# Attention with shared keys: the last key tile's exponentials enter the summing product directly

## The reference, cut to what matters

```
def blocked_attention(q, k, v, scale):
    ...
        s = jnp.einsum('bqhgd,bkhd->bhgqk', qblk, k, preferred_element_type=jnp.float32) * scale
        p = jax.nn.softmax(s, axis=-1)
        return jnp.einsum('bhgqk,bkhd->bqhgd', p.astype(v.dtype), v)
...
        o = jnp.concatenate([
            blocked_attention(qm, ..., MLA_SCALE),
            blocked_attention(qg, ..., GQA_SCALE)], axis=-1)
```

## Time and profile before

| | |
|---|---|
| median of 3 runs | 3780.42 us (3778.26 to 3781.32) |
| the profiled execution, by the same clock as the runs | 3788.75 us |
| its span, first to last instruction | 3787.0 us |
| PE busy | 3304.8 us (87%) |
| DVE busy | 2715.6 us (72%) |
| ACT busy | 1853.9 us (49%) |
| mean granted TensorE clock | 0.936 |

### The profile page before, as it was taken

The page is one execution under the profiler, slowest core; times in us unless marked ns, Lnnn a source line. Parts: engine busy times, 40 slices in busy tenths (PEclk is TensorE's granted clock), DMA queues, the critical chain, the costliest instruction groups (busy, mean ns, idle before and its releaser), DMA issues. The chain is left out here.

```text
span 3787.0 us, 44337 instructions
## 1 busy us (share of the span) xinstructions
PE 3304.8 (87%) x14416; PEld 2224.1 (59%) x14416; DVE 2715.6 (72%) x2841; ACT 1853.9 (49%) x2125; POOL 1456.2 (38%) x1091
## 2 busy tenths in 40 slices
PE   6999699999695999999959996999978599999990
PEld 2555355544384788888824443555437488887870
DVE  1444466677586899989856654777767698988997
ACT  0222233344310888888823332333331188888881
POOL 2111011121111877777721110111121287777771
PEclk9999799999896999999979997999999699999995
DMA  8465532211441998798754336221115278997974
GB/s 339 157 233 186 157 94 67 58 48 37 143 150 71 404 365 309 275 350 321 298 210 135 124 102 181 73 64 43 40 39 196 98 292 336 349 363 284 353 276 195
DMA packets 258758, 739.56 MB, mean 195 GB/s; under 512 B 55456, under 2 KB 149440, under 8 KB 205272
## 3 DMA queue, kind: packets, MB, share of 16 engines
q0 software_dynamic: 114288, 528.57, 36.4%
q1 hardware_dynamic: 129816, 157.73, 13.7%
q10 hardware_dynamic: 14544, 51.92, 3.8%
HBM read 723.62 MB, written 129.61 MB: 225 GB/s over the span
## 5 line engine op out<-in xcount | busy, mean ns | idle before, releaser
L2033 DVE TENSOR_TENSOR ex_wl<-ex_wr,ex_wh 128x2048 fp32r<-128x2048 f32 x440 | 988.0, 2285 | 63.9 <-ACT ex_wh L1978 63.8
L1978 ACT ACTIVATE ex_wh<-ex_wr 128x2048 fp32r<-128x2048 f32 x440 | 843.1, 1916 | 77.4 <-PE ex_yp L1941 55.1
L1185 ACT ACTIVATE at_pt<-at_st 128x1024 f32<-128x1024 f32 (+1 forms) x336 | 336.5, 1003 | 552.7 <-PE at_st L1120 550.0
L1231 DVE TENSOR_REDUCE at_nm<-at_sc 128x1 f32<-128x1280 f32 (+1 forms) x276 | 378.3, 1371 | 216.1 <-PE at_sc L1085 213.6
L764 PE MATMUL zp<-w_in,hT 128*128 128x480 f32 x960 | 428.8, 580 | 31.5 <-DVE hT L539 21.6
L1245 DVE TENSOR_TENSOR at_acc<-at_acc,at_pt 128x1024 f32<-128x1024 f32 x256 | 318.2, 1243 | 94.6 <-ACT at_pt L1185 92.4
L1859 POOL DMA_INDIRECT ex_wr<-in_w_down,piece_of x152 | 315.6, 2077 | 46.3 <-issue 46.0
L1134 PE MATMUL at_op<-at_pt,at_va 128*64 128x512 f32 (+1 forms) x1344 | 318.6, 603 | 0.2
L1120 PE MATMUL at_st<-at_q,at_km 96*128 96x512 f32 (+3 forms) x1008 | 266.2, 404 | 16.6 <-DMA at_q<-at_nmT 14.6
L764 PEld LDWEIGHTS zp<-w_in,hT 128*128 128x128 f32 x960 | 173.5, 195 | 180.2 <-issue 168.5
L1120 PEld LDWEIGHTS at_st<-at_q,at_km 96*128 96x128 f32 (+1 forms) x1008 | 180.6, 193 | 104.0 <-issue 42.6
(11 more groups left out here) (281 smaller groups left out, 5941.2 us busy)
## 6 DMA issues: line engine op xcount, KB each, us to landing
ad_w<-in_w_ada POOLq DMA_DIRECT2D x48, 1024.0 KB, 10.4
q_mla<-qT SPq DMA_DIRECT2D x40, 384.0 KB, 3.8
k_mla<-kT SPq DMA_DIRECT2D x40, 384.0 KB, 5.7
at_km<-k_mla SPq DMA_DIRECT2D x16, 960.0 KB, 12.0
at_q<-q_mla SPq DMA_DIRECT2D x32, 384.0 KB, 11.6
w_in<-in_w_in SPq DMA_DIRECT2D x6, 1920.0 KB, 25.5
q_gqa<-gqT SPq DMA_DIRECT2D x20, 512.0 KB, 6.8
cy<-y_s POOLq DMA_DIRECT2D x10, 1024.0 KB, 7.1
```

The lines of the kernel that those rows point to most:

```text
L1185: nc.scalar.activation(pt[:, j % PT, :, 0:nq], st[:, j % 2, :, 0:nq], ACT.Exp).then_inc(exp_done, 1)
L1231: nc.vector.tensor_reduce(nm[:, v % 3, s:s + 1], score_bank(A_NO[v, s])[:, 0:kb * P], AX.X, ALU.max, negate=True).then_inc(max_done, 1)
L1978: nc.scalar.activation(wh[:, q], wr[:, u, p], ACT.Copy).then_inc(hi_done, 1)
L2033: nc.vector.tensor_tensor(wl[:, q], wr[:, u, p], wh[:, q].bitcast(F32), ALU.subtract).then_inc(lo_done, 1)
```

## The change

It concerns the latent units of the GQA pairs, 8 in each layer, 16 in all. In them the tenth key tile (k = 9) is no longer added to `acc` on DVE. Instead `sums` has two parts that accumulate in the same PSUM bank: ones times `acc` (tiles 0 to 8), and ones times the tenth tile of `pt` itself. In all units `sums` waits in addition for the unit's last exponential. ACT's wait before it overwrites that tile of the ring is now for `r_full`, the end of `sums`, instead of for an addition.

```diff
+        def direct(u):
+
+            return U[u][0] >= G0 and U[u][3] == NT
+
         def sums_done(u):
 
-            return sum(unit[3] - 1 for unit in U[:u + 1])
+            return sum(U[w][3] - (2 if direct(w) else 1) for w in range(u + 1))
...
                 pe.wait_ge(acc_done, sums_done(u))
                 pe.wait_ge(op_taken, u + 1)
-                for h in range(2):
-                    ins = nc.tensor.matmul(op[VD * h:VD * h + VD, 0:nq], C["ones"][:, 0:VD], acc[:, u % 2, h, 0:nq], start=True, stop=True)
+                pe.wait_ge(exp_done, AT[u + 1])
+                parts = [acc[:, u % 2]] + ([pt[:, (AT[u + 1] - 1) % PT]] if direct(u) else [])
+                for n, part in enumerate(parts):
+                    for h in range(2):
+                        ins = nc.tensor.matmul(op[VD * h:VD * h + VD, 0:nq], C["ones"][:, 0:VD], part[:, h, 0:nq],
+                                               start=(n == 0), stop=(n == len(parts) - 1))
                 ins.then_inc(r_full, 1)
...
-                    act.wait_ge(acc_done, sums_done(w - 1) + max(j - PT - AT[w], 1))
+                    i = j - PT - AT[w]
+                    if direct(w) and i == U[w][3] - 1:
+                        act.wait_ge(r_full, w + 1)
+                    else:
+                        act.wait_ge(acc_done, sums_done(w - 1) + max(i, 1))
...
-                    if k > 0:
+                    if k > 0 and not (direct(u) and k == U[u][3] - 1):
                         accumulate(u, k)
```

## The result

The changed kernel takes 3798.85 us as the median of its runs, against 3779.5 us for the kernel before, measured beside it. The ratio is 1.0046 (95% interval 1.0035 to 1.0058), so it is 13.2 to 21.9 us slower, 17.4 us by the middle. The prediction was 3794.2 us, 13.8 us slower. One execution of 11699.35 us is left out of the ratio; the median of the remaining five is 3798.1 us.

A forecast was written before the change was run, and what follows sets the result against it. PE was taken to bound the path at the sums, with DVE waiting for it. Addition removed 0, product 16 x 0.86 = 13.8 us, waits 0, on 3780.42 us gives 3794.2 us; range 3788.5 to 3798.5 us.

The forecast's parts named there:

- part 1: DVE's ninth addition in 16 GQA latent units: removing 1.22 us each, 19.5 us of work, gains 0.
- part 2: Two more products in each of 16 units' sums on PE: 0.86 us a unit, bounds 0.58 and 1.08 us.
- The matmul records' own 592 ns: Rival at the new products: the two heads do not overlap, 2.37 us a unit, 37.9 us in all; chance 0.03.
- the four FP32 passes: Skill's rule for the new products: 0.86 us per product, 1.73 us a unit, 27.6 us in all, giving 3808.0 us.
- The rival that it hides in PE's waits: PE's 1.9 us idle per unit absorbs the product: 3780.4 us, or 3787.3 us if hidden in layer 0 only; chance 0.05.
- the wait that was to stay near 0.66 us: Sign in the profile after: PE's wait before the sixth `begin` of a GQA latent unit still near 0.66 us.
- part 3: Sums' third wait on PE and ACT's changed wait: 0 each; 0.8 us for 40 units kept for the range.
- The sum: Forecast total over the GQA latent units: 16 units x 0.86 us = 13.8 us slower, 3794.2 us.
- the unit with a clock of 0.94: GQA latent unit read as 28.50 against 28.51 us; rival that half the units get that clock: 3807.0 us, chance 0.03.

The follow-up runs named there:

- the second one: The changed kernel run once more, nothing altered, against the kernel before: ratio 1.0053 (1.0039 to 1.0067), 20 us slower.
- two tiles direct: Changed kernel with key tile 8 as well as 9 going straight into the sums, seven additions instead of eight: 1.0069 against the kernel before, 26 us slower.
- zeros in key tile 2: Kernel before plus four zero-weight matmul records behind the values in key tile 2 of the 16 GQA latent units: ratio 1.0038, 14.4 us slower.
- the wait alone: Kernel before with only the third wait, for the unit's last exponential, ahead of the sums in all 40 units: ratio 1.0000 (0.9991 to 1.0009).
- spreading the values: Kernel before, GQA latent units: values of key tiles 2, 3, 4 done one each in key tiles 3, 4, 5, not all in 5: ratio 0.9976.
- key tile 7 moved: Kernel before with values of key tiles 2, 3, 4 spread and those of key tile 7 done in 9 instead of 8: ratio 0.9958.

## Why the prediction was right

**The addition was free** (part 1). Confirmed three times: with it kept beside the product the unit is 29.33 to 29.44 us, with it on POOL layer 1's unit is 28.52 us, and DVE's idle time took its place. At layer 1's end it gained nothing either (21.35 and 21.37 us between the last two sums).

**The price of the product, 0.86 us a unit** (part 2). Confirmed: 29.37 us for 28.51, 30.22 to 30.27 us with two tiles, 29.34 to 29.38 us for four records of zeros. The matmul records' own 592 ns would have given 2.37 us. Differences between groups of 4, 8 and 12 records gave the right price. In the trace the four new records start in two pairs, 0.43 us apart, so two run at a time in the new place as well. Of the Trainium skill's two rules the one of "TensorEngine Tiling (Array Packing)", that different tiles can execute in parallel (Tiling Modes, Key Properties), fits; the four FP32 passes one after another for each head would have given 1.73 us by that estimate, and the unit grew by half of it. That the two that run together are the two heads is not shown: the records do not name the head, and no run has one head alone.

**Nothing hides it, because of where it stands.** The rival that it hides in PE's waits was right that such waits can hide it, and wrong about the place. The same four records cost 14.4 us between key tiles 2 and 3 and 2.3 us behind key tile 3.

One sign is miscounted: the wait that was to stay near 0.66 us stands before the seventh `begin` (key tile 4), not the sixth. It stayed.

**The waits** (part 3) show no cost, measured by themselves.

**What remains open is a size, 3.6 us.** The sum was 13.8 us; the measurement's interval is 13.2 to 21.9 us, which holds it, and that of the second one 14.7 to 25.3, which starts 0.9 us above it. Both have their middle above the sum. The kernels with two tiles direct (26 us for 27.5) and with zeros in key tile 2 (14.4 for 13.8) show no such excess. The candidate was the clock, for which the sum has no term. I wrote that the unit with a clock of 0.94 was no longer for it. That was a misreading: in the earlier trace rows I had cut the stretch at a fixed 28.50 us. Cut from sums to sums it is this:

```profile
2719.84:2749.97 30.13, 28.29 (x111) 14.35 (x110) 22.28 (x18) 11.47 (x14) 4.54 (x7) 0.94 0.06 19
```

It lasted 30.13 us, 1.6 us longer. The number of such losses differs between executions: in both GQA stretches 5.1 us for the kernel before and 1.7 us for the wait alone; 8.5, 1.7 and 6.8 us for the two executions of the changed kernel and the one with the addition kept; 0 us for two tiles direct. That two tiles cost 26 us and not 31 would fit a loss of none, but that is one execution of five. The table as a whole speaks against the candidate: six profiled executions with the product or the zeros of key tile 2 lost 4.6 us on average (0 to 8.5), the other six 4.3 us (0 to 10.2). So a loss can move one execution by 10 us, but that the change draws more of them is not shown. The cause of the 3.6 us stays open; and since the interval reaches down to 13.2 us, the excess itself is not certain.

## What to carry to other kernels

Before moving work from one engine to another, find which engine ended each wait just ahead of and just behind both places: here the addition had 2 us of idle time behind it and the product none in front of it or behind it, up to the next maximum. Price pipelined matmuls by the distance from group to group, with groups of different length, never by the records' own durations, and price a wait in the same way, from start to start. And if an engine has waits, move existing work into them first: spreading the values added no instruction and gave 9 us, 16 us with key tile 7 moved as well, where the change lost 17.

## What the runs showed of the hardware that I had not expected

- The granted clock fell to 0.50 for some 3.4 us in units where a plain one has PE busy for 27.5 of 29.4 us. In layer 1 it fell at the second of two waits of about 0.66 and 0.75 us in 14 of 15 cases, and in most units with these waits it did not fall. Each time cost 1.6 to 1.7 us; in the two GQA stretches together there were none to six of them in an execution.
- A wait of PE that the profile shows as 0.38 us cost 0.67 us from start to start.
- A POOL addition of 128 x 1024 float32 takes 2.36 us, against 1.22 us on DVE; PE waited for it only in layer 0, where POOL's queue held it back (1.65 us of PE's waiting at one sums).
- The kernel that altered the attention output in key tile 2 had 168 matmul records more, and was 35 us slower in its span (3832.9 us) than the one that adds the same four records a unit with weights of zero (3797.5 us).
